# The 42 projection units: split once in the first block, stored as high and low parts, loaded by the other three blocks

## The reference, cut to what matters

```python
proj = h @ w_in                       # 1024 x (768 attn | 1536 deltanet | 8 | 512 z | 2048 gates)
y_attn = o_attn @ w_branch[:512]
y_dn   = o_dn @ w_branch[512:]
merged = sigmoid(gate_a) * y_attn + sigmoid(gate_d) * y_dn
x = x + gate1 * (merged @ w_out)
x = x + gate2 * swiglu(rms_norm(x) * (1 + scale2) + shift2, w_gate_up, w_down)
```

## Time and profile before

| what | value |
|---|---|
| time, median of 3 runs | 2879.8 us (2879.57 to 2880.38) |
| the profiled execution's own time | 2879.23 us |
| its span, first to last instruction | 2877.3 us |
| mean granted TensorE clock | 0.995 |
| PE busy | 2830.7 us, 98% |
| DVE busy | 1815.7 us, 63% |
| ACT busy | 1239.3 us, 43% |
| DMA | 523.51 MB, mean 182 GB/s |

### The profile page before, as it was taken

The page is one execution under the profiler, slowest core; times in us unless marked ns, Lnnn a source line. Parts: engine busy times, 40 slices in busy tenths (PEclk is TensorE's granted clock), DMA queues, the critical chain, the costliest instruction groups (busy, mean ns, idle before and its releaser), DMA issues.

```text
span 2877.3 us, 39886 instructions
## 1 busy us (share of the span) xinstructions
PE 2830.7 (98%) x14954; PEld 2331.7 (81%) x14954; DVE 1815.7 (63%) x3122; ACT 1239.3 (43%) x2232; POOL 133.3 (5%) x124
## 2 busy tenths in 40 slices
PE   8999999999999999999999999999999999999999
PEld 6887888977877888888889877788778888888887
DVE  5876576875687666658876666665757622223686
ACT  4654545554444333334445554365544311112343
POOL 0011000010020000000000110000100100000000
PEclk9999999999999999999999999999999999999999
DMA  7443354533448787886433334424243676777743
GB/s 289 157 147 107 121 165 132 187 95 115 142 165 311 291 296 291 298 332 207 140 116 111 120 94 136 154 82 156 78 140 121 218 242 232 245 245 264 299 136 102
DMA packets 222512, 523.51 MB, mean 182 GB/s; under 512 B 43249, under 2 KB 43505, under 8 KB 213361
## 3 DMA queue, kind: packets, MB, share of 16 engines
q1 hardware_dynamic: 173056, 423.39, 44.8%
q10 hardware_dynamic: 49264, 97.57, 8.9%
HBM read 362.03 MB, written 158.86 MB: 181 GB/s over the span
## 4 chain that ended last, share of the span: by engine, by line
PE 85%; DVE 7%; ACT 3%; DMA 2%; DVEq 2%; issue 1%; SPq 1%; POOL 0%; ACTq 0%
PE gb L2457 26%; PE mb L2501 22%; PE gb L2501 19%; PE gb L2882 5%; PE gb L2487 4%; PE mb L2726 2%; PE mb L2699 1%; PE mb L2721 1%; PE mb L2627 1%; ACT sc L1364 1%; DVE tmp_c L2068 1%; DVE w_lo L1616 1%; DVE inv_c L2071 1%; PE mb L2792 1%; DVE a_mx L2052 1%
## 5 line engine op out<-in xcount | busy, mean ns | idle before, releaser
L2457 PE MATMUL gb<-h_hi,w_hi 128*128 128x512 f32 x1024 | 408.2, 399 | 4.1 <-DVE w_lo L1616 3.5
L2457 PE MATMUL gb<-h_lo,w_hi 128*128 128x512 f32 x1024 | 406.2, 397 | 0.0
L2457 PE MATMUL gb<-h_hi,w_lo 128*128 128x512 f32 x1024 | 406.2, 397 | 0.0
L2501 PE MATMUL mb<-t_hi,fw_both 128*128 128x512 f32 x1056 | 349.9, 393 | 9.2 <-DVE t_lo L1794 5.1
L1616 DVE TENSOR_TENSOR w_lo<-w_raw,w_hi 128x1024 fp32r<-128x1024 f32 x216 | 262.7, 1219 | 80.1 <-ACT w_hi L1074 79.1
L1074 ACT ACTIVATE w_hi<-w_raw 128x1024 fp32r<-128x1024 f32 x216 | 227.9, 1055 | 87.7 <-PE gb L2882 40.9
L2501 PEld LDWEIGHTS mb<-t_hi,fw_both 128*128 128x128 f32 x1056 | 199.9, 189 | 54.5 <-DVE t_lo L1794 7.8
L2457 PEld LDWEIGHTS gb<-h_hi,w_hi 128*128 128x128 f32 x1024 | 192.9, 188 | 53.2 <-issue 7.3
L2457 PEld LDWEIGHTS gb<-h_lo,w_hi 128*128 128x128 f32 x1024 | 193.1, 189 | 42.8 <-issue 5.3
L2457 PEld LDWEIGHTS gb<-h_hi,w_lo 128*128 128x128 f32 x1024 | 192.9, 188 | 40.3
L2501 PE MATMUL gb<-td_hi,fw_both 128*128 128x512 f32 x704 | 219.7, 390 | 0.3 <-DVE td_lo L1783 0.2
(11 more groups left out here) (370 smaller groups left out, 5966.2 us busy)
## 6 DMA issues: line engine op xcount, KB each, us to landing
w_raw<-in_wstream SPq DMA_DIRECT2D x216, 512.0 KB, 3.6
scratch_parts<-fw_both ACTq DMA_DIRECT2D x154, 512.0 KB, 4.1
fw_both<-scratch_parts SPq DMA_DIRECT2D x154, 512.0 KB, 4.7
scratch_hid<-spill SPq DMA_DIRECT2D x22, 1792.0 KB, 7.4
td_raw<-scratch_hid SPq DMA_DIRECT2D x154, 256.0 KB, 3.0
ada_buf<-in_ada_w SPq DMA_DIRECT2D x24, 1024.0 KB, 7.7
w_raw<-in_wgate SPq DMA_DIRECT2D x34, 512.0 KB, 8.2
wq<-in_wdown SPq DMA_DIRECT2D x8, 1280.0 KB, 11.3
```

Of the source, the lines that this page charges most:

```text
L2457: last = pe.matmul(bank(j), w, r, start=(i == 0), stop=(i == n - 1))
L2501: done = pe.matmul(out, w, (lo if part == 1 else hi)[:, tile, :] if tile is not None else (lo if part == 1 else hi), start=(first and part ...
```

## The change

Units 12 to 53 of blocks 1, 2 and 3 ("kept" units, `is_kept`) are no longer loaded raw and split. In block 0 these 42 units are loaded and split as before, and ACT then stores both parts to a DRAM buffer `park_u`, two DMAs of 512 KB per unit, two units later in its order. Block 0's split of unit g now also waits, before it overwrites slot g % 3, until the stored unit g - 3 has landed in DRAM. In blocks 1 to 3 ACT's `split` of a kept unit waits for `unit_used` alone and then issues two DMAs of 512 KB into `w_hi` and `w_lo`; DVE's `split` and SP's `load_unit` return at once. TensorE waits for the landing of both DMAs instead of `w_ready`. Units 0 to 11 stay as they were in all blocks. The waits of SP that were counted in `w_ready` (the first loads of a block, and the first three gate-weight loads after block 1) now name the last unit that was split.

```diff
+def is_kept(g):
+    return g >= U_PER and g % U_PER >= U_AT
+def splits_to(g):
+    return sum(not is_kept(i) for i in range(g + 1))
...
+    park_u = nc.dram_tensor("scratch_units", (U_PER - U_AT, P, 2, UW), fp32, kind="Internal").ap()
...
+    def kept_landed(b, u):
+        k = (5, 4, None)[slot(b, u)]
+        n = (b - 1) * KEPT_PER_SLOT * 32 + 32 * ((u - U_AT) // RING + 1)
+        if k is None:
+            return sin_done, 2 + n
+        return raw_in[k], n + (gate_loads[k] + 16 * slots[k] if b >= 2 else 0)
...
 (SP)        def load_unit(b, u):
-                sp.wait_ge(w_ready.sem, b * U_PER + (u + 1))
-                s = slot(b, u)
+                g, s = b * U_PER + u, slot(b, u)
+                if is_kept(g):
+                    return
+                former = [i for i in range(s, g, RING) if not is_kept(i)][-1]
+                sp.wait_ge(w_ready.sem, w_ready.at(0, splits_to(former)))
...
 (ACT)       def split(b, u):
-                act.wait_ge(w_loaded[s], 16 * ((b * U_PER + u) // RING + 1))
                 unit_used(b, u - RING)
+                if is_kept(b * U_PER + u):
+                    if b == 1 and u == U_AT:
+                        for last in range(U_PER - RING, U_PER):
+                            act.wait_ge(*store_landed(last))
+                    act.dma_start(w_hi[s][:, :].bitcast(fp32), park_u[u - U_AT][:, 0, :]).then_inc(kept_landed(b, u)[0], 16)
+                    act.dma_start(w_lo[s][:, :].bitcast(fp32), park_u[u - U_AT][:, 1, :]).then_inc(kept_landed(b, u)[0], 16)
+                    return
+                act.wait_ge(w_loaded[s], 16 * (sum(not is_kept(i) for i in range(s, b * U_PER + u + 1, RING))))
...
+                if U_AT <= b * U_PER + u - RING < U_PER:
+                    act.wait_ge(*store_landed(b * U_PER + u - RING))
                 act.activation(w_hi[s][:, :], w_raw[s][:, :], ACT.Copy).then_inc(w_high.sem, 1)
+                if U_AT + 2 <= b * U_PER + u < U_PER + 2:
+                    store_unit(b * U_PER + u - 2)
+
+            def store_unit(g):
+                s = g % RING
+                act.wait_ge(w_ready.sem, w_ready.at(0, splits_to(g)))
+                act.dma_start(park_u[g - U_AT][:, 0, :], w_hi[s][:, :].bitcast(fp32)).then_inc(unit_out[s].sem, 16)
+                act.dma_start(park_u[g - U_AT][:, 1, :], w_lo[s][:, :].bitcast(fp32)).then_inc(unit_out[s].sem, 16)
...
 (DVE)       def split(b, u):
+                if is_kept(g):
+                    return
...
 (PE)
+            def parts_there(b, u):
+                g = b * U_PER + u
+                if is_kept(g):
+                    pe.wait_ge(*kept_landed(b, u))
+                else:
+                    pe.wait_ge(w_ready.sem, w_ready.at(0, splits_to(g)))
```

More of the change, by code:

```diff
@@ L152 @@
 LAST_USE, HALVES = last_uses()
+def is_kept(g):
+    return g >= U_PER and g % U_PER >= U_AT
+def splits_to(g):
+    return sum(not is_kept(i) for i in range(g + 1))
+KEPT_PER_SLOT = (U_PER - U_AT) // RING
+assert U_AT % RING == 0
 ADA_FIRST, ADA_TURNS = 4, 12
@@ L608, in layer_program @@
     uses = [[n for n in range(N_GATE) if part_slot(1, n) == k] for k in range(PARTS)]
[L609 to L612, removed]
+    unit_in = [KEPT_PER_SLOT * 32 if k >= 4 else 0 for k in range(6)]
+    per_raw = [16 * (slots[k] + len(uses[k])) + 2 * unit_in[k] for k in range(6)]
+    f_loaded = [Signal(raw_in[k], per_raw[k], unit_in[k]) for k in range(4)]
+    t_loaded = [Signal(raw_in[k], per_raw[k], unit_in[k] + gate_loads[k]) for k in range(6)]
+    parts_in = [Signal(raw_in[k], 0, 3 * unit_in[k] + gate_loads[k] + 16 * slots[k]) for k in range(6)]
+    def kept_landed(b, u):
[4 more added lines that the diff above has]
+        return raw_in[k], n + (gate_loads[k] + 16 * slots[k] if b >= 2 else 0)
     t_high, t_ready = sig("t_high", N_DOWN_STEPS), sig("t_ready", N_DOWN_STEPS)
@@ L634, in layer_program, with store_landed @@
     spilled = Signal(zeroed, 16 * NPAIR, 16 * 2 * NT)
+    unit_out = [Signal(sem, 0, 1) for sem in (c_silu, picks_set, picks_summed)]
     parts_out = [Signal(sem, 0, before) for sem, before in (
-        (c_silu, 1), (ada_kept, len(ADA_ROWS)), (nea_exp, 1), (picks_set, 1), (picks_summed, 1), (ada_rows, len(ADA_ROWS)))]
+        (c_silu, 1 + KEPT_PER_SLOT * 32), (ada_kept, len(ADA_ROWS)), (nea_exp, 1), (picks_set, 1 + KEPT_PER_SLOT * 32),
+        (picks_summed, 1 + KEPT_PER_SLOT * 32), (ada_rows, len(ADA_ROWS)))]
+    def store_landed(u):
+        return unit_out[u % RING].sem, unit_out[u % RING].at(0, 32 * ((u - U_AT) // RING + 1))
     def parts_count(n):
@@ L840, in _ @@
                             if v < 3:
-                                sp.wait_ge(w_ready.sem, w_ready.at(b, U_OUT + 6 + v))
+                                sp.wait_ge(w_ready.sem, w_ready.at(0, splits_to(b * U_PER + U_AT - RING + v)))
                             elif v == 3:
@@ L1614, in split @@
                     return
-                dve.wait_ge(w_high.sem, b * U_PER + (u + 1))
+                g = b * U_PER + u
+                if is_kept(g):
+                    return
+                dve.wait_ge(w_high.sem, w_high.at(0, splits_to(g)))
                 dve.tensor_tensor(w_lo[s][:, :], w_raw[s][:, :], w_hi[s][:, :].bitcast(fp32), ALU.subtract
@@ L2450, in by_feature @@
                 if first == 0:
-                    pe.wait_ge(w_ready.sem, w_ready.at(b, u + 1))
+                    parts_there(b, u)
                     free_bank(b, j)
```

## The result

The changed kernel takes 2926.6 us, the median of four runs (2925.52 to 2927.81), against 2879.7 for the kernel before on the same chip. The ratio is 1.0162, with a 95% interval from 1.0151 to 1.0174: 46.9 us slower. The forecast was 2888, its range ended at 2900. The direction was right and the size was not.

What follows compares the result with a forecast made beforehand. TensorE was taken to bound the kernel, busy 2830.7 of 2877.3 us. Losses of 17.9 less gains of 8.4 gave +9.5 on 2879.2, so 2888.7, less 1 for overlap: 2888 us, range 2872 to 2900.

Steps and rivals of the forecast that it cites:

- the one for the images: Blocks 1 to 3: image transfers start earlier, so two thirds of TensorE's waits for them go, 3.0 us won.
- the slow stretches: Half-clock stretches behind the image waits, 1.7 us in block 1 and 3.4 in block 2: half go, 2.5 us won.
- if the waits of the image stage stay: One of the signs named in advance that would show the prediction wrong; it expected these waits shorter in blocks 1 to 3.
- The same step for block 0: Block 0's image stage: stores of units 28 to 30 run beside the image transfers, 3 us lost, bounds 0 and 8.
- Unit 47: Blocks 1 to 3: its pair is issued late and lands after 5.0 us, a new TensorE wait, 7.2 us lost.
- 7.2 + 3.1 + 1.0: Losses in us: the wait at unit 47, the slow clock behind it, and units 48 and 49 of each block.
- six in ten: Chance of a slow-clock stretch of 1.7 us behind each new gap at unit 47, 3.1 us lost for three blocks.
- Unit 39: Blocks 1 to 3: its pair shares the queues with the four xs loads, 1.0 us each, 3.0 us lost.
- Units 30 and 31: Blocks 1 to 3: unit 30 loses 0.2 us each; unit 31's wait of 0.56 us goes, 1.7 us won.
- t_o: DVE's split of unit 39 before t_o is gone, so TensorE's wait there shrinks: 1.2 us won, bounds 0 and 2.4.
- Cost in TensorE's time 0: Block 0: ACT stops for stores at about ten places, only PSUM copies queue behind, so TensorE loses nothing.
- Contention: Rival: 63 MB more loads and 44 MB more stores collide with xs, x1 and images: 2903 us or more, chance 0.10.

Runs made afterwards that it cites:

- the version that beats both: Changed kernel with only units 22 to 31 kept, unit 31's pair issued before end_inverse, block 0's stores of units 29 and 30 before it too: 2874.2 us.
- the run with half of the bytes: Changed kernel, but part loads of units 30 to 33 in blocks 1 to 3 move 64 of 128 partitions, with as many DMAs: 2920.7 us.

## Why the prediction was wrong in size

**The step that failed** is the one for the images: "of their waits in blocks 1 to 3 ... I take two thirds, 3.0 us won, bounds 0 and 4.5, because unit 31's megabyte now runs beside the image writes", and with it "half, 2.5 us won" of the slow stretches. Its premise nearly held: the inversion ended 2.4 to 2.6 us earlier against unit 30, where it had taken 3. But the megabyte that it mentions was priced as a discount on a gain, unit 32's megabyte, which crosses the image loads, was not named at all, and a loss was left out of the bounds. It was a loss: 17.7 us in blocks 1 to 3, where the forecast had won 5.5, because the way from the inversion's end to lc_u grew from 9.7 to 10.4 us to 14.8 to 15.1. The forecast's own sign of being wrong, "if the waits of the image stage stay", came true. The same step for block 0 ("2 us and a longer slow stretch of 1 us") had the mechanism and took 3 for what measured 7.6. The forecast looked at who starts the chain of transfers, not at what the chain meets. It had also taken the wait for the images as a prize; the version that beats both shows that closing it uncovers a wait for DVE's copy of about the same length.

What the trace had to say: before, a raw tile had a place of its own and was loaded far ahead. In block 1 the raw loads of units 31 and 32 had landed at 620.9 and 628.0 us, ahead of the first image write at 633.72, and unit 33's went out at 642.35, behind lc_u in SP's written order; none met the images before lc_u was issued. A kept unit's pair overwrites the parts of unit g - 3, so it can't leave before TensorE has finished that unit, and it goes on ACT's queue, where nothing orders it against SP's. The page's view of the queues over the nine microseconds from the first write shows it, first the changed kernel (651.5 to 660.5 us; q10 carries ACT's loads, q1 is SP's), then the version that beats both (631.4 to 640.4 us); columns are packets, MB, share of the engines:

```profile
DMA packets 1326, 1.66 MB, mean 185 GB/s; under 512 B 948, under 2 KB 948, under 8 KB 1326
...
q10 hardware_dynamic: 415, 1.55, 56.4%
q1 hardware_dynamic: 911, 0.11, 8.1%
```

```profile
q1 hardware_dynamic: 2954, 0.79, 47.1%
q10 hardware_dynamic: 166, 0.56, 15.4%
```

SP's packets are the small ones: 0.11 MB in 911 makes some 120 bytes each, and 948 of all are under 512 bytes. In the same nine microseconds 911 of SP's packets came through instead of 2954 (there lc_u and part of a raw load are among them already). The Trainium skill, "DMA: Bandwidth & Descriptors", section on queues, rings and completion order, says that a DMA engine takes turns between the queues that have work, a packet at a time; a packet there is several descriptors, so it need not be what the profile counts as one. By that, SP's small packets wait in turn for ACT's large ones, and the delay goes with how many of those are in flight; the run with half of the bytes agrees (3 us too much in place of 5). That the turns are the reason was not measured by itself.

**Unit 47 was right**: 5.15 us from issue to start against 5.0 taken, 7.0 us by the starts of unit 47 against 7.2, and 10.1 us at units 47 to 49 in blocks 1 to 3 against 7.2 + 3.1 + 1.0 = 11.3. The clock fell behind it once in three, where six in ten were taken. **Unit 39** cost 2.9 us (3.0 taken). **Units 30 and 31** won 4.2 (1.7 less 0.6 taken). **t_o**: TensorE came to unit 38 1.1 us earlier (1.2 taken), though the wait in the view shrank by 0.4 alone.

**Block 0** was the second miss. "Cost in TensorE's time 0" for ACT's stops forgot what stands behind a split on DVE: `h_lo` at the turn to block 1, 4.0 us, and `mod_g` at unit 17, 4.2 us, where the loads of the modulation weights slow the stores that ACT waits for. 2.2 us came at units 47 to 49, with a new wait of 1.6 us for the norm's `n_rs` that was not followed further. The forecast had looked at the copies out of PSUM that ACT makes, not at DVE's order behind ACT.

**The rivals.** Contention, "2903 or more", with a chance of 0.10, is what came, though with the largest part in a place that it did not price: it spoke of pairs of 8 us at units 47 and 39, and had the images in passing. Its own terms add up to 36 us, that is 2915, and not to 2903. The range ended at 2900, so it left this rival out. The failed terms account for the miss, in the traces 47.8 us against 9.5: images 28, block 0 without them 13 (3 of it chance), units 30, 31 and the rest about -3.

## What to carry to other kernels

Splitting once and loading both parts trades engine time for DMA traffic; here TensorE ends the time and neither DVE nor ACT does, and the first 61 us of relief (33 of DVE, 28 of ACT, the ten units up to the end of the inversion) were worth 6.5 us, the next 58 us nothing. When transfers move to another engine's queue, list what they can now meet that the old queue's order kept apart, and above all chains of small transfers; give the term for each meeting a bound on the losing side. When a wait is added on an engine, follow it through the order of the next engine too, and not only to the instructions behind it on its own. And before calling a wait a prize, look for the next wait that stands close behind it.

## What the runs showed of the hardware

- Four writes of 16 KB each held SP for 1.53 us undisturbed and for 4.06 us with 512 KB loads of another queue in flight; the issue of lc_u took 1.71 us instead of 0.59.
- A pair of 512 KB loads issued 0.36 us apart on ACT's queue landed after 4.1 and 5.3 us in the median, but after 6.9 and 9.1 us behind 2 MB of x1 and 2 MB of gate weights.
- Gaps of TensorE of 5.1 to 5.4 us at the images each came with 10.2 us at 1.2 GHz, which began before the gap ended, though TensorE was busy for 8.1 to 9.7 us of them. Gaps of 0.22 and 0.31 us were followed by full clock, also past the gaps of 1.8 us that came 7 us later. In the kernel before, gaps of 1.25, 1.92 and 1.31 us were followed by 3.4, 6.8 and 0 us at 1.2 GHz, so the gap's length alone does not tell. A wait of 5 us was in part paid a second time: the starts of unit 32 slipped by 5.7, 4.2 and 7.8 us while the waits had grown by 4.0, 3.2 and 4.1.
